# Two transformer blocks on one core: reordering the end of the first stage, with part of the next stage's modulation sums on GpSimd

## The chip, the cores and the metric

The kernel runs on one core of one Trainium2 chip. The metric is the device time of one execution in microseconds (us), given as the median of three runs; shorter is better. PE is TensorE, PEld its weight loads, DVE VectorE, ACT ScalarE, POOL GpSimd, SP SyncE (here only a queue of DMAs).

## The reference, cut to what matters

A block of a token mixer and a SwiGLU feed-forward, then a second model of two layers with three sublayers each, on 256 tokens of width 1024, all in f32. Each of the eight sublayers is modulated by a vector computed from `c`: shift, scale and gate are `silu(c) @ w_ada + b_ada`. The part that the change touches is the first sublayer, from its convolution and its attention to the layer norm behind it, and the modulation vector of the second:

```python
u = gate_c * hc
conv = sum(conv_w[j] * pad(u)[:, j:j + s, :] for j in range(3))
conv_out = group_rms_norm(gate_b * conv, conv_norm_g, 8)
attn = group_rms_norm(sparse_indexer_attention(q, k, v, qi, ki, wi, 64), attn_norm_g, 8)
mix = concat([attn, conv_out]) @ w_out
x = layer_norm(2**0.25 * x + g1 * mix, ln1_g, ln1_b)
ff = swiglu(modulate(x, sh2, sc2), w_gate, w_up, w_down)      # sh2, sc2 = part of silu(c) @ w_ada
```

## The kernel before, in words

The whole program is one launch of eight stages, `s` = 0 to 7, one for each sublayer. Every engine has its own instruction stream, written out by hand in the order in which it runs; semaphores alone tie the streams together. There is no planner.

Weights stream through a ring of three slots of 128x2048 f32 (a unit). SP loads a unit into `raw`, ACT rounds it to `whi` (`hi`, L674), DVE takes the rest into `wlo` (`lo`, L1294), and PE multiplies three times for each product (`three`, L2157: high by high, high by low, low by high). The inputs are split in the same way into `hhi` and `hlo`. A unit may be loaded once the `lo` three units before it is done. Stage 0 has 14 units, called U to U+13 here; U+10 to U+13 are the output projection `w_out`, each with 24 matmuls of 512 columns, 12 for each half of the tokens (t = 0 and 1).

The modulation vector of stage 1 (its shift and scale) and the gate of stage 0 are summed outside PE: 24 pieces (128 rows of `w_ada`, 1024 columns each) are loaded by POOL (`early_piece`, L551 to L557) into five slots in turn, and DVE multiplies each by a column of `silu(c)` and adds it to `ada_acc` (`early_piece`, L1619 to L1628, one instruction of 128x1024). Pieces 0 to 7 belong to the gate, 8 to 23 to stage 1. The semaphore `a_used` counts finished pieces; a piece's slot is loaded again when the piece five before it is done. At the end PE adds up the 128 rows of `ada_acc` with a matrix of ones (`sum_gate`, `sum_columns`, L2165: 16 column sums, 32 PE instructions), once all 24 pieces are in.

The end of stage 0 runs as follows.

- DVE forms `u` (L1752, `conv_u`) when PE has finished unit U+9. ACT multiplies it by the last tap (L1245, `conv_tap`), DVE adds the other two taps in a chain of eight instructions (L1761) and multiplies by the gate (L1763, `conv_gated`), ACT squares (L1250, `conv_sq`), PE sums the groups (L2850, `group_mm`), DVE scales (L1768, `block_mean`), POOL takes the inverse root (`inverse_root`, L494, `block_root`), PE turns it (L2856), ACT copies it (L1255, `group_out`), PE spreads it over the features (L2862, `spread_mm`), and DVE normalises (L1780, `mix_f`).
- Beside that the attention ends. PE turns the softmax weights (`turn_weights`, L2817), ACT and DVE copy them out (L1219, L1739), PE multiplies by the values (`attend(t)`, L2827), ACT squares (L1214), DVE sums and takes the means (`heads_out`), POOL the inverse root, DVE normalises (`heads_norm`, L1731), PE turns (the transposes in front of `output_product`, L2282), and DVE multiplies by the gain (L1787, `mix_f`).
- Each third of the mixed input is split by ACT (L712) and DVE (L1347). PE then runs `output_product`: unit U+10 for both t, then, in `close`, `sum_gate(0)`, U+11 to U+13 for t = 0, then U+11 to U+13 for t = 1. `sum_columns(1)` follows.
- DVE in `leave_first` (L1414): multiplies by the gate and takes the moments of t = 0 (L1356, L1371, L1376), adds pieces 21 to 23, runs `lo` of the next stage's first unit, sets the columns of stage 1 (L1325 to L1328) when PE has summed them, modulates, and does t = 1.

`keep_busy(n, b)` (L2151) issues n matmuls of ones into bank b, two PE instructions each; their result is not used.

Of the kernel before, what the change touches and what calls it, by code (L numbers as in the profile page):

```python
# [26 lines left out]
ALU = mybir.AluOpType  # L27
# [124 lines left out]
def two_blocks(  # L152
# [30 lines left out]
    with ExitStack() as ctx:  # L183
# [146 lines left out]
        q_copied, vg_out, lv_sub, lv_exp, lv_mul = sem("q_copied"), sem("vg_out"), sem("lv_sub"), sem("lv_exp"), sem("lv_mul")  # L330
        lv_mm, lv_copy, g_silu = sem("lv_mm"), sem("lv_copy"), sem("g_silu")
        lv_far, o_scaled = sem("lv_far"), sem("o_scaled")
        mean_eps, hi_first, lo_first = sem("mean_eps"), sem("hi_first"), sem("lo_first")

        def linked(engine, own):
# [155 lines left out]
        def _(pool):  # L491
# [101 lines left out]
            for s in range(NSUB):  # L593
# [11 lines left out]
                if s == 0:  # L605
                    pool.wait_ge(f_used, 13)
                    pool.wait_ge(w_hi, 2)
                    pool.wait_ge(cols_sum, 1)
                    for n in range(13):
                        early_piece(n)  # L610
                    pool.wait_ge(block_mean, 1)
                    inverse_root(st[:, 40:56], 16, block_root)
                    early_piece(13)
                    pool.wait_ge(block_mean, 2)
                    inverse_root(st[:, 120:128], 8, block_root)
                    early_piece(14)
                    pool.wait_ge(block_mean, 3)
                    inverse_root(st[:, 128:136], 8, block_root)
                    for n in range(15, EARLY):
                        early_piece(n)  # L620
                elif s == 1:

                    pool.wait_ge(toe_rows, 1)
                    pool.dma_start(bias_row[:, :], big[0:HEADS, 2560:2560 + TOE]).then_inc(toe_land, 16)
                elif s == 2:

                    rows = big[:, 3072:3072 + HEADS * TOE]
                    ada_pieces(s, 0, 5)
                    pool.wait_ge(toe_land, 48)
                    pool.dma_start(rows, bias_row.rearrange("h j -> (h j)").unsqueeze(0).to_broadcast((P, HEADS * TOE))).then_inc(toe_land, 16)  # L630
                    ada_pieces(s, 5, 6)
                    pool.wait_ge(toe_land, 64)
                    pool.dma_start(bias_rows[:, :, :], rows.rearrange("p (h j) -> p h j", h=HEADS)).then_inc(toe_land, 16)
                    ada_pieces(s, 6, 7)
                    pool.wait_ge(toe_land, 80)
                    skewed = bass.AP(tensor=bias_rows.tensor, offset=bias_rows.offset + P - 1,
                                     ap=[[HEADS * TOE - 1, P], [TOE, HEADS], [1, TOK]])
                    pool.dma_start(big[:, 6144:8192].rearrange("p (h k) -> p h k", h=HEADS), skewed).then_inc(toe_land, 16)
                    ada_pieces(s, 7, KT)
# [25 lines left out]
        def _(sc):  # L665
# [572 lines left out]
            exps(0)  # L1238
            hi(U + 11)
            exps(1)  # L1240
            take_turned(0)
            sc.wait_ge(conv_u, 1)
            sc.wait_ge(w_used, used(U + 7))
            for ct in range(4):
                done = sc.activation(hf[:, ct, :], big[:, D + ct * TOK:D + (ct + 1) * TOK], ACT.Copy,  # L1245
                                     scale=vec[:, V_CW + 8 + ct:V_CW + 9 + ct])
            done.then_inc(conv_tap, 1)
            square_heads_out(0)
            sc.wait_ge(conv_gated, 1)
            sc.activation(hfl[:, 0:D], hfl[:, D:2 * D], ACT.Square).then_inc(conv_sq, 1)  # L1250
            take_turned(1)
            square_heads_out(1)
            hi(U + 12)
            sc.wait_ge(group_tr, 1)
            sc.activation(act[0:8, 0, 0:TOK], ps[0:8, 1, 0:TOK], ACT.Copy).then_inc(group_out, 1)  # L1255
            split_mixed(1, 4, 4, 0, TOK)
            for t in range(NT):
                split_mixed(2 + t, 0, 4, t * P, P)
# [18 lines left out]
        def _(ve):  # L1277
# [468 lines left out]
            choose(1)  # L1746
            logits(0)
            lo(U + 9)
            logits(1)
            ve.wait_ge(w_used, used(U + 9))  # L1750
            ve.wait_ge(hc_out, 1)
            ve.tensor_tensor(big[:, D:2 * D], big[:, 0:D], bank(2, 2), ALU.mult).then_inc(conv_u, 1)  # L1752
            early_piece(7)
            lo(U + 10)
            early_piece(8)

            ve.wait_ge(conv_tap, 1)
            for ct in range(4):
                for j in (1, 2):
                    w = V_CW + 4 * (2 - j) + ct  # L1760
                    link(ve.scalar_tensor_tensor(cv[:, ct, j:TOK], u[:, ct, 0:TOK - j], vec[:, w:w + 1], cv[:, ct, j:TOK],  # L1761
                                                 ALU.mult, ALU.add))
            ve.tensor_tensor(hfl[:, D:2 * D], hfl[:, 0:D], bank(0, 2), ALU.mult).then_inc(conv_gated, 1)  # L1763
            early_piece(9)
            pt_evac(1)
            early_piece(10)
            ve.wait_ge(group_mm, 1)
            ve.tensor_scalar(st[:, 40:56], ps[:, 0, 0:16], 1.0 / 64, EPS1, ALU.mult, ALU.add).then_inc(block_mean, 1)  # L1768
            heads_out(0)
            early_piece(11)  # L1770
            lo(U + 11)
            early_piece(12)
            heads_out(1)
            heads_norm(0)
            early_piece(13)
            heads_norm(1)

            ve.wait_ge(spread_mm, 1)
            for ct in range(4):
                done = ve.scalar_tensor_tensor(hf[:, 4 + ct, :], hf[:, 4 + ct, :], vec[:, V_CG + ct:V_CG + ct + 1],  # L1780
                                               psf[:, ct * TOK:(ct + 1) * TOK], ALU.mult, ALU.mult)
            done.then_inc(mix_f, 1)
            early_piece(14)
            split_mixed(1, 4, 4, 0, TOK)
            for t in range(NT):
                ve.wait_ge(o_tr, t + 1)
                ve.tensor_tensor(hf[:, 0:4, t * P:(t + 1) * P], ps[:, 4 + t, :].rearrange("p (k n) -> p k n", k=4),  # L1787
                                 vec[:, V_AG:V_AG + 4].unsqueeze(2).to_broadcast((P, 4, P)), ALU.mult).then_inc(mix_f, 1)
                split_mixed(2 + t, 0, 4, t * P, P)
            ve.wait_ge(lam_exp, 1)  # L1790
            link(ve.tensor_tensor(st[:, 220:221], st[:, 219:220], st[:, 218:219], ALU.subtract))
            link(ve.tensor_scalar(st[:, 221:222], st[:, 220:221], -LAMBDA_INIT, None, ALU.add))
            lo(U + 12)
            for n in range(15, 19):
                early_piece(n)
            lo(U + 13)
            early_piece(19)
            early_piece(20)
            leave_first()

            def attention():
# [345 lines left out]
        def _(pe):  # L2147
# [110 lines left out]
            def close(s, places, before):  # L2258

                last = len(places) - 1  # L2260
                for j, place in enumerate(places):
                    before(j, 0)
                    done = rows_of(*place, 0, False, j == last, signal=y_ready if j == last else None)
                done.then_inc(y_ready, 1)
                for j, place in enumerate(places):
                    turning = (lambda: transpose_inputs(s + 1, 0)) if j == last and s in (2, 4, 5) else None
                    before(j, 1)
                    if j == last and s in (3, 6):
                        transpose_inputs(s + 1, 0)
                    rows_of(*place, 1, False, j == last, signal=y_ready if j == last else None,  # L2270
                            between=turning).then_inc(w_used, 1)
                if s == 0:
                    sum_columns(1)
                if s == 1:
                    sum_columns(2)
                if s < 2:
                    transpose_inputs(s + 1, 0)
# [32 lines left out]
            def output_product(s, unit, mixed_ready, k0=0, beside=None):  # L2310
# [10 lines left out]
                        pe.wait_ge(mix_lo, mixed_ready[j, t])  # L2321

                def before(j, t):
                    if s == 0 and (j, t) == (0, 0):
                        pe.wait_ge(mix_f, 3)
                        sum_gate(0)
                    mixed(j + 1, t)
# [490 lines left out]
                                            logit_rows(t)[:, h, g * P:(g + 1) * P], ident)  # L2818
                done.then_inc(p_tr, 1)

            def attend(t):
                pe.wait_ge(pt_s, t + 1)
                if t:
                    pe.wait_ge(pt_v, 1)
                for h in range(HEADS):
                    for g in range(t + 1):
                        done = pe.matmul(ps[:, (2, 6)[t], h * 64:(h + 1) * 64], PT[:, g, h * P:(h + 1) * P],  # L2827
                                         tok[:, g, VO:VO + 64], start=g == 0, stop=g == t)
                done.then_inc(pv_mm, 1)

            pe.wait_ge(qT_out, 1)
            logit_products(0)
# [6 lines left out]
            keep_busy(4, 4)  # L2839
            pe.wait_ge(conv_u, 1)  # L2840
            turn_weights(0)
            keep_busy(5, 5)
            attend(0)
            turn_weights(1)
            keep_busy(8, 3)

            pe.wait_ge(conv_sq, 1)
            for t in range(NT):
# [1 line left out]
                    done = pe.matmul(ps[:, 0, 8 * t + 2 * ct:8 * t + 2 * ct + 2], hf[:, ct, t * P:(t + 1) * P],  # L2850
                                     kc[:, C_HALF:C_HALF + 2], start=True, stop=True)
            done.then_inc(group_mm, 1)
            attend(1)
            pe.wait_ge(block_root, 1)
            for t in range(NT):
                done = pe.transpose(ps[0:8, 1, t * P:(t + 1) * P], st[:, 40 + 8 * t:48 + 8 * t], ident)  # L2856
            done.then_inc(group_tr, 1)
            keep_busy(7, 3)
            pe.wait_ge(group_out, 1)
            pe.wait_ge(spread_land, 16)  # L2860
            for ct in range(4):
                done = pe.matmul(psf[:, ct * TOK:(ct + 1) * TOK], gate[0:8, 1, ct * P:(ct + 1) * P], act[0:8, 0, 0:TOK],  # L2862
                                 start=True, stop=True)
            done.then_inc(spread_mm, 1)
            for t in range(NT):
                pe.wait_ge(o_done, t + 1)
                transposes([big[:, 3920 + BANK * t + j * P:3920 + BANK * t + (j + 1) * P] for j in range(4)], 4 + t, o_tr)
            output_product(0, U + 10, {(0, 0): 1, (2, 0): 2, (2, 1): 3}, 4)

            for s in range(1, NSUB):  # L2870
                if s in SWIGLUS:
# [28 lines left out]
```

## Time and profile before

| | |
|---|---|
| median of 3 runs | 1447.03 us (1443.84 to 1448.16) |
| the profiled execution | 1452.88 us |
| its span, first to last instruction | 1451.2 us |
| mean granted TensorE clock | 0.979 |
| busy: PE / PEld / DVE / ACT / POOL | 1414.5 / 1184.0 / 1051.4 / 705.8 / 180.4 us |

The change touches the stretch from about 97 us to about 183 us of the span. The busy share of an engine is a mean over the whole span, and eight stages behind that stretch are the same code before and after. So the page serves to find the stretch, and the chain of waits, the timelines of the engines and the clock within it say what a change there is worth.

### The profile page before, as it was taken

The numbers are of one execution on the slowest core, as the hardware profiler recorded it, in microseconds if no ns is written. First come the engines' busy times: TensorE is split into PE (matmuls) and PEld (weight loads), VectorE is DVE, ScalarE is ACT, GpSimd is POOL, SyncE is SP. The second block draws the span as 40 slices with busy tenths as digits, with TensorE's granted clock in tenths as the row PEclk, the third lists the DMA queues.
The fourth block names the chain that finished last, engine by engine and source line by source line (L and its number), as shares of the span: only waits on it lengthen the run. The fifth ranks groups of instructions, "written<-read, shape, count | busy, mean of one in ns | idle before, by whom it ended". The sixth has DMA issues, their size and how long they took to land.

```text
span 1451.2 us, 19791 instructions
## 1 busy us (share of the span) xinstructions
PE 1414.5 (97%) x7136; PEld 1184.0 (82%) x7136; DVE 1051.4 (72%) x1105; ACT 705.8 (49%) x936; POOL 180.4 (12%) x272
## 2 busy tenths in 40 slices
PE   8998999999999999999999999999999999999998
PEld 8897778888788887768788887788888988788887
DVE  5888867776768877686667775688866888665555
ACT  2453354444634335667734345534338856644342
POOL 3103111110301210211101101111101001100000
PEclk7996999999999999999999999999999999999999
DMA  9846479897389995443578983899955342466661
GB/s 356 317 146 203 146 240 307 307 312 255 118 292 349 367 361 192 149 156 107 194 269 313 316 280 113 287 336 343 344 184 180 117 140 88 131 205 227 222 228 59
DMA packets 187526, 335.62 MB, mean 231 GB/s; under 512 B 9169, under 2 KB 123453, under 8 KB 187216
## 3 DMA queue, kind: packets, MB, share of 16 engines
q1 hardware_dynamic: 160528, 237.95, 48.7%
q0 software_dynamic: 26736, 96.71, 18.4%
q8 instruction: 35, 0.57, 0.2%
q10 hardware_dynamic: 208, 0.23, 0.0%
q14 instruction: 19, 0.16, 0.0%
HBM read 332.23 MB, written 2.63 MB: 231 GB/s over the span
## 4 chain that ended last, share of the span: by engine, by line
PE 78%; DVE 10%; issue 4%; ACT 3%; DMA 3%; POOL 1%; SPq 1%; DVEq 0%; ACTq 0%; POOLq 0%
PE ps L2157 68%; DMA raw<-in_ffn_w_in 2%; DVE wlo L1294 2%; PE ps L2165 1%; PE ps L2351 1%; PE ps L2612 1%; PE ps L2282 1%; DVE ada_acc L1627 1%; DMA big<-in_w_ada 1%; DVE xn L1356 1%; ACT whi L674 1%; POOL st L494 1%; PE ps L2296 1%; ACT hf L699 1%; DVE xs L1361 1%
## 5 line engine op out<-in xcount | busy, mean ns | idle before, releaser
L1294 DVE TENSOR_TENSOR wlo<-raw,whi 128x2048 fp32r<-128x2048 f32 x203 | 463.3, 2285 | 145.0 <-ACT whi L674 143.7
L2157 PE MATMUL ps<-whi,hhi 128*128 128x512 f32 (+1 forms) x1208 | 490.8, 406 | 13.3 <-DVE hlo L1347 4.2
L674 ACT ACTIVATE whi<-raw 128x2048 fp32r<-128x2048 f32 x208 | 396.4, 1909 | 218.0 <-PE ps L2157 163.9
L2157 PE MATMUL ps<-whi,hlo 128*128 128x512 f32 (+1 forms) x1208 | 475.5, 394 | 0.0
L2157 PE MATMUL ps<-wlo,hhi 128*128 128x512 f32 (+1 forms) x1208 | 474.7, 393 | 0.0
L2157 PEld LDWEIGHTS ps<-whi,hhi 128*128 128x128 f32 x1208 | 229.8, 190 | 67.0 <-issue 8.2
L2157 PEld LDWEIGHTS ps<-whi,hlo 128*128 128x128 f32 x1208 | 229.4, 190 | 49.6
L2157 PEld LDWEIGHTS ps<-wlo,hhi 128*128 128x128 f32 x1208 | 230.2, 191 | 45.1 <-issue 1.7
L2157 PE MATMUL ps<-whi,ahi 128*128 128x512 f32 x400 | 156.2, 390 | 0.7 <-DVE alo L1514 0.7
L2157 PE MATMUL ps<-whi,alo 128*128 128x512 f32 x400 | 155.7, 389 | 0.0
L2157 PE MATMUL ps<-wlo,ahi 128*128 128x512 f32 x400 | 155.6, 389 | 0.0
L1309 DVE SCALAR_TENSOR_TENSOR ada_acc<-ada_raw,csil,ada_acc 128x1024 f32<-128x1024 f32 x104 | 130.3, 1278 | 0.0
L527 POOL DMA_DIRECT2D ada_raw<-in_ada_w x96 | 51.1, 532 | 542.9 <-DVE ada_acc L1309 531.3
L792 ACT ACTIVATE ahi<-ps 128x512 fp32r<-128x512 f32 x50 | 29.9, 599 | 181.7 <-PE ps L2351 181.7
L788 ACT ACTIVATE act<-ps 128x256 f32<-128x256 f32 x110 | 42.1, 384 | 146.7 <-PE ps L2157 146.5
L1514 DVE TENSOR_TENSOR alo<-ps,ahi 128x512 fp32r<-128x512 f32 x50 | 34.6, 692 | 88.9 <-ACT ahi L792 88.8
L2157 PEld LDWEIGHTS ps<-whi,ahi 128*128 128x128 f32 x400 | 75.1, 188 | 16.5 <-DVE wlo L1294 1.1
L2157 PEld LDWEIGHTS ps<-whi,alo 128*128 128x128 f32 x400 | 75.1, 188 | 15.6
L2157 PEld LDWEIGHTS ps<-wlo,ahi 128*128 128x128 f32 x400 | 75.1, 188 | 15.4
L494 POOL TENSOR_TENSOR st<-st 128x1 f32<-128x1 f32 (+3 forms) x35 | 41.7, 1192 | 205.1 <-DVE st L1393 64.6
L1509 DVE TENSOR_TENSOR act<-act,ps 128x256 f32<-128x256 f32 x110 | 42.7, 416 | 29.8 <-ACT act L788 29.6
L2157 PE MATMUL ps<-hhi,whi 128*128 128x256 f32 x224 | 64.2, 287 | 0.0
(288 smaller groups left out, 1496.5 us busy)
## 6 DMA issues: line engine op xcount, KB each, us to landing
raw<-in_ffn_w_in SPq DMA_DIRECT2D x176, 512.0 KB
ada_raw<-in_ada_w POOLq DMA_DIRECT2D x96, 512.0 KB, 5.2
raw<-in_ffn_w_down SPq DMA_DIRECT2D x44, 1024.0 KB
big<-in_ada_w POOLq DMA_DIRECT2D x48, 512.0 KB, 6.2
raw<-in_hgrn_w_in SPq DMA_DIRECT2D x16, 1024.0 KB
raw<-in_attn_w_qkv SPq DMA_DIRECT2D x12, 1024.0 KB
ada_raw<-in_w_ada POOLq DMA_DIRECT2D x23, 512.0 KB, 4.9
raw<-in_w_gate SPq DMA_DIRECT2D x22, 512.0 KB
```

What stands on the lines that cost most here:

```text
L494: pool.tensor_tensor(cols, cols, half.to_broadcast((P, width)), ALU.pow).then_inc(signal, 1)
L527: pool.dma_start(ada_slot(p), w[bass.ds(kt * P, P), first + j * D:first + (j + 1) * D])\
L674: sc.activation(whi[:, slot, 0:n], raw[:, slot, 0:n], ACT.Copy).then_inc(w_hi, 1)
L699: done = sc.activation(hf[:, kt, toks], ps[:, 2 * t + kt // 4, kt % 4 * P:(kt % 4 + 1) * P], ACT.Identity, scale=modc[:, s % 2, 8 + kt:9 + ...
L788: sc.activation(act[:, t, :], ps[:, 4 + t, 0:FC], ACT.Silu).then_inc(silu_done, 1)
L792: sc.activation(ahi.rearrange("p k n -> p (k n)"), bank(6), ACT.Copy).then_inc(ahi_ready, 1)
L1294: ve.tensor_tensor(wlo[:, slot, 0:n], raw[:, slot, 0:n], whi[:, slot, 0:n].bitcast(F32), ALU.subtract)\
L1309: ve.scalar_tensor_tensor(acc, ada_slot(p), csil[:, bass.ds((0 if a < 2 else 8) + kt, 1)], acc, ALU.mult, ALU.add).then_inc(a_used, 1)
L1356: link(ve.tensor_tensor(xn[:, t, cols], bank(2 * t + h), gate[:, s % 2, cols], ALU.mult))
L1509: ve.tensor_tensor(act[:, t, :], act[:, t, :], ps[:, 4 + t, FC:2 * FC], ALU.mult).then_inc(act_ready, 1)
L1514: ve.tensor_tensor(a_lo, bank(6), a_hi.bitcast(F32), ALU.subtract).then_inc(alo_ready, 1)
L2157: done = pe.matmul(dst, lhsT, rhs, start=first and n == 0, stop=final and n == 2, skip_group_check=True)
```

## The change

In stage 0's end and in the step to stage 1:

1. DVE. Pieces 7 and 8 move ahead of the forming of `u`, to either side of `logits(1)`. The chain of taps follows `lo(U+10)` at once, and waits for each of ACT's four taps by itself. Piece 9 moves behind the copy of the turned weights, piece 10 behind `heads_out(0)`, piece 12 behind the normalised convolution, where it was 14. `heads_out(1)`, `heads_norm(1)` and the second third of the input move behind the split of the convolution's part. `lo(U+12)` moves between the two steps of the last third. Pieces 17 to 20 leave DVE.
2. POOL. It issues the load of piece 13 before it waits for the first mean, and 14 and 15 one step earlier too. Behind its three inverse roots it issues 16 to 21, and then multiplies and adds pieces 17, 18, 19 and 20 itself, in two instructions each (a product in place, then a sum, with a semaphore between), issuing the loads of 22 and 23 between them.
3. ACT. The four taps come before the copy of the first turned weights; the squares for t = 1 come behind `group_out`; the copy of the second turned weights comes before the convolution's square.
4. PE. `turn_weights(1)` comes before `attend(0)`; `attend(1)` is cut in two, four heads before and four behind the spreading; three groups of `keep_busy` go or change size (5, 8 and 7 matmuls out, 10 in); `keep_busy(5)` is new in front of `sum_columns(1)`.
5. PE. The output product starts once the heads of t = 0 are turned. The heads of t = 1 are turned between U+10 and U+11, and `sum_gate(0)` moves from before U+11 to before U+12.

```diff
@@ gpsimd
-                    for n in range(13):
+                    for n in range(14):
                         early_piece(n)
                     pool.wait_ge(block_mean, 1)
                     inverse_root(st[:, 40:56], 16, block_root)
-                    early_piece(13)
+                    early_piece(14)
                     pool.wait_ge(block_mean, 2)
                     inverse_root(st[:, 120:128], 8, block_root)
-                    early_piece(14)
+                    early_piece(15)
                     pool.wait_ge(block_mean, 3)
                     inverse_root(st[:, 128:136], 8, block_root)
-                    for n in range(15, EARLY):
+                    for n in range(16, 22):
                         early_piece(n)
+                    for n in range(17, 21):
+                        pool.wait_ge(a_land[n % EARLY_SLOTS], 16 * (n // EARLY_SLOTS + 1))
+                        pool.wait_ge(a_used, n)
+                        kt, j = divmod(n - KT, 2)
+                        acc = ada_acc[:, 1, j * D:(j + 1) * D]
+                        pool.tensor_scalar(early_slot(n % EARLY_SLOTS), early_slot(n % EARLY_SLOTS), csil[:, kt:kt + 1], None,
+                                           ALU.mult).then_inc(piece_scaled, 1)
+                        pool.wait_ge(piece_scaled, n - 16)
+                        pool.tensor_tensor(acc, acc, early_slot(n % EARLY_SLOTS), ALU.add).then_inc(a_used, 1)
+                        if n + EARLY_SLOTS < EARLY:
+                            early_piece(n + EARLY_SLOTS)
@@ scalar
             exps(1)
-            take_turned(0)
             sc.wait_ge(conv_u, 1)
             sc.wait_ge(w_used, used(U + 7))
             for ct in range(4):
-                done = sc.activation(hf[:, ct, :], ...)
-            done.then_inc(conv_tap, 1)
+                sc.activation(hf[:, ct, :], ...).then_inc(conv_tap, 1)
+            take_turned(0)
             square_heads_out(0)
+            take_turned(1)
             sc.wait_ge(conv_gated, 1)
             sc.activation(hfl[:, 0:D], hfl[:, D:2 * D], ACT.Square).then_inc(conv_sq, 1)
-            take_turned(1)
-            square_heads_out(1)
             hi(U + 12)
             sc.wait_ge(group_tr, 1)
             sc.activation(act[0:8, 0, 0:TOK], ps[0:8, 1, 0:TOK], ACT.Copy).then_inc(group_out, 1)
+            square_heads_out(1)
             split_mixed(1, 4, 4, 0, TOK)
@@ vector
             lo(U + 9)
+            early_piece(7)
             logits(1)
+            early_piece(8)
             ...
             ve.tensor_tensor(big[:, D:2 * D], big[:, 0:D], bank(2, 2), ALU.mult).then_inc(conv_u, 1)
-            early_piece(7)
             lo(U + 10)
-            early_piece(8)
-            ve.wait_ge(conv_tap, 1)
             for ct in range(4):
+                ve.wait_ge(conv_tap, ct + 1)
                 ...
+            pt_evac(1)
             early_piece(9)
-            pt_evac(1)
-            early_piece(10)
             ve.wait_ge(group_mm, 1)
             ...
             heads_out(0)
+            early_piece(10)
             early_piece(11)
             lo(U + 11)
-            early_piece(12)
-            heads_out(1)
             heads_norm(0)
-            early_piece(13)
-            heads_norm(1)
             ve.wait_ge(spread_mm, 1)
             ...
-            early_piece(14)
+            early_piece(12)
             split_mixed(1, 4, 4, 0, TOK)
-            for t in range(NT): (L1787 and split_mixed of t)
+            heads_out(1)
+            turned_heads(0)
+            early_piece(13)
+            split_mixed(2, 0, 4, 0, P)
+            heads_norm(1)
+            early_piece(14)
+            early_piece(15)
+            turned_heads(1)
+            lo(U + 12)
+            split_mixed(3, 0, 4, P, P)
             ...
-            lo(U + 12)
-            for n in range(15, 19):
-                early_piece(n)
+            early_piece(16)
             lo(U + 13)
-            early_piece(19)
-            early_piece(20)
             leave_first()
@@ tensor
                 if s == 0:
+                    keep_busy(5, column_bank(1))
                     sum_columns(1)
@@
-                    if s == 0 and (j, t) == (0, 0):
+                    if s == 0 and (j, t) == (1, 0):
                         pe.wait_ge(mix_f, 3)
                         sum_gate(0)
@@
             turn_weights(0)
-            keep_busy(5, 5)
-            attend(0)
             turn_weights(1)
-            keep_busy(8, 3)
+            pe.wait_ge(pt_s, 1)
+            attend(0, range(HEADS)).then_inc(pv_mm, 1)
+            keep_busy(10, 3)
             ...
-            attend(1)
+            attend(1, range(4))
             pe.wait_ge(block_root, 1)
             ...
-            keep_busy(7, 3)
             pe.wait_ge(group_out, 1)
             ...
             done.then_inc(spread_mm, 1)
-            for t in range(NT): (wait for o_done, transposes)
-            output_product(0, U + 10, {(0, 0): 1, (2, 0): 2, (2, 1): 3}, 4)
+            attend(1, range(4, HEADS)).then_inc(pv_mm, 1)
+            turn_heads_out(0)
+            output_product(0, U + 10, {(0, 0): 1, (2, 0): 2, (2, 1): 3}, 4, beside_first)
```

`beside_first` calls `turn_heads_out(1)` at (1, 0), before U+11 of t = 0; `turned_heads(t)` is the wait for the turned heads and L1787.

## Rows read from the trace of the kernel before

**Rows 1.** The page's part 4, the chain that ended last, by engine.

```profile
PE 78%; DVE 10%; issue 4%; ACT 3%; DMA 3%; POOL 1%; SPq 1%; DVEq 0%; ACTq 0%; POOLq 0%
```

**Rows 2.** Chain of waits, 118 to 199 us: start, us, engine, tile, line, count.

```profile
118.62 1.23 DVE hf L1763
...
119.88 1.06 ACT hf L1250
...
120.99 3.03 PE ps L2850 x16
124.02 6.93 PE ps L2827 x32
...
131.37 2.99 PE ps L2151 x14
134.36 3.72 PE ps L2862 x8
...
167.76 3.85 PE ps L2165 x32
...
183.07 15.48 PE ps L2157 x60
```

**Rows 3.** Timeline of DVE; in brackets the idle time before and its releaser.

```profile
108.74 1.22 DVE L1752 TENSOR_TENSOR big<-big,ps 128x1024 f32<-128x1024 f32 x1 [1.25 <-PE ps L2157]
...
111.08 2.28 DVE L1294 TENSOR_TENSOR wlo<-raw,whi 128x2048 fp32r<-128x2048 f32 x1
...
114.48 4.11 DVE L1761 SCALAR_TENSOR_TENSOR hf<-big,vec,hf 128x255 f32<-128x255 f32 x8
...
138.10 1.66 DVE L1780 SCALAR_TENSOR_TENSOR hf<-hf,vec,ps 128x256 f32<-128x256 f32 x4 [1.95 <-PE ps L2862]
...
159.58 0.69 DVE L1371 SCALAR_TENSOR_TENSOR xs<-xs,xn 128x512 f32<-128x512 f32 x1
...
166.42 1.28 DVE L1627 SCALAR_TENSOR_TENSOR ada_acc<-ada_acc,csil 128x1024 f32<-128x1024 f32 x1
```

**Rows 4.** Timeline of ACT, same columns.

```profile
112.38 1.69 ACT L1245 ACTIVATE hf<-big,vec 128x256 f32<-128x256 f32 x4
...
130.98 0.60 ACT L1214 ACTIVATE xn<-ps 128x512 f32<-128x512 f32 x1 [9.13 <-PE ps L2827]
...
139.79 1.06 ACT L712 ACTIVATE hhi<-hf 128x1024 fp32r<-128x1024 f32 x1 [6.16 <-DVE hf L1780]
```

**Rows 5.** Timeline of PE, same columns.

```profile
112.53 2.00 PE L2827 MATMUL ps<-big 128*128 128x64 f32 x16 [0.30 <-ACT big L1219]
...
116.12 1.95 PE L2151 MATMUL ps<-ones 128*128 128x128 f32 x16
...
142.17 0.79 PE L2157 MATMUL ps<-whi,hhi 128*128 128x512 f32 x1 [2.20 <-DVE hlo L1347]
...
167.19 0.39 PE L2157 MATMUL ps<-whi,hlo 128*128 128x512 f32 x1
```

**Rows 6.** Windows: us, busy of PE, PEld, DVE, ACT, POOL; PEclk, DMA share, GB/s.

```profile
120.00:130.00 10.00, 9.01 (x45) 9.01 (x46) 9.18 (x12) 1.85 (x2) 5.65 (x3) 0.58 0.48 141
130.00:140.00 10.00, 9.97 (x37) 8.04 (x36) 6.21 (x16) 2.86 (x4) 4.96 (x7) 0.50 0.84 279
140.00:150.00 10.00, 7.83 (x26) 6.14 (x27) 8.41 (x10) 2.54 (x4) 0.53 (x1) 0.72 0.47 163
```

**Rows 7.** Timeline of POOL, 124 to 181 us, columns as for DVE.

```profile
124.31 2.94 POOL L494 TENSOR_TENSOR st<-st 128x16 f32<-128x16 f32 x1 [12.33 <-DVE st L1768]
...
163.70 1.60 POOL L494 TENSOR_TENSOR st<-st 128x1 f32<-128x1 f32 x1 [8.74 <-DVE st L1393]
165.40 1.03 POOL L582 TENSOR_SCALAR st<-st 128x1 f32<-128x1 f32 x1
...
179.76 0.56 POOL L494 TENSOR_TENSOR st<-st 128x1 f32<-128x1 f32 x1 [13.34 <-DVE st L1393]
```

**Rows 8.** Groups of POOL by line and shape: busy us, mean ns, idle before.

```profile
L512 POOL MEMSET ada_acc<- 128x1024 f32 x1 | 1.0, 957 | 0.0
```

More of the change, by code:

```diff
@@ L332, in two_blocks @@
         lv_far, o_scaled = sem("lv_far"), sem("o_scaled")
+        piece_scaled = sem("piece_scaled")
         mean_eps, hi_first, lo_first = sem("mean_eps"), sem("hi_first"), sem("lo_first")
@@ L1244, in _ @@
             for ct in range(4):
-                done = sc.activation(hf[:, ct, :], big[:, D + ct * TOK:D + (ct + 1) * TOK], ACT.Copy,
-                                     scale=vec[:, V_CW + 8 + ct:V_CW + 9 + ct])
-            done.then_inc(conv_tap, 1)
+                sc.activation(hf[:, ct, :], big[:, D + ct * TOK:D + (ct + 1) * TOK], ACT.Copy,
+                              scale=vec[:, V_CW + 8 + ct:V_CW + 9 + ct]).then_inc(conv_tap, 1)
+            take_turned(0)
             square_heads_out(0)
+            take_turned(1)
             sc.wait_ge(conv_gated, 1)
             sc.activation(hfl[:, 0:D], hfl[:, D:2 * D], ACT.Square).then_inc(conv_sq, 1)
-            take_turned(1)
-            square_heads_out(1)
             hi(U + 12)
@@ L1782, in _, with turned_heads @@
             done.then_inc(mix_f, 1)
-            early_piece(14)
+            early_piece(12)
             split_mixed(1, 4, 4, 0, TOK)
-            for t in range(NT):
+            def turned_heads(t):
                 ve.wait_ge(o_tr, t + 1)
@@ L1788, in _ @@
                                  vec[:, V_AG:V_AG + 4].unsqueeze(2).to_broadcast((P, 4, P)), ALU.mult).then_inc(mix_f, 1)
-                split_mixed(2 + t, 0, 4, t * P, P)
+            heads_out(1)
[8 more added lines that the diff above has]
+            split_mixed(3, 0, 4, P, P)
             ve.wait_ge(lam_exp, 1)
@@ L2819, in turn_weights, with attend @@
                 done.then_inc(p_tr, 1)
[L2821 to L2825, printed above, removed]
+            def attend(t, heads):
+                for h in heads:
                     for g in range(t + 1):
@@ L2828, in attend @@
                                          tok[:, g, VO:VO + 64], start=g == 0, stop=g == t)
-                done.then_inc(pv_mm, 1)
+                return done
             pe.wait_ge(qT_out, 1)
@@ L2852, in _ @@
             done.then_inc(group_mm, 1)
-            attend(1)
+            pe.wait_ge(pt_s, 2)
+            pe.wait_ge(pt_v, 1)
+            attend(1, range(4))
             pe.wait_ge(block_root, 1)
@@ L2864, in _, with turn_heads_out, beside_first @@
             done.then_inc(spread_mm, 1)
-            for t in range(NT):
+            attend(1, range(4, HEADS)).then_inc(pv_mm, 1)
+            def turn_heads_out(t):
                 pe.wait_ge(o_done, t + 1)
                 transposes([big[:, 3920 + BANK * t + j * P:3920 + BANK * t + (j + 1) * P] for j in range(4)], 4 + t, o_tr)
-            output_product(0, U + 10, {(0, 0): 1, (2, 0): 2, (2, 1): 3}, 4)
+            def beside_first(j, t):
+                if (j, t) == (1, 0):
+                    turn_heads_out(1)
+            turn_heads_out(0)
+            output_product(0, U + 10, {(0, 0): 1, (2, 0): 2, (2, 1): 3}, 4, beside_first)
             for s in range(1, NSUB):
```

## The prediction

> **What bounds the kernel now.** The chain of waits is read first. Over the whole span it is PE for 78% [rows 1], so a change counts only where PE waits or runs slowly. The stretch that the change rewrites holds both. From 118.6 to 140 us the chain alternates: gate product on DVE, square on ACT, group sums, the second `attend` (6.93 us), `keep_busy` (2.99) and the spreading (3.72) on PE [rows 2], then the normalising on DVE, for which it had waited 1.95 us [rows 3]. Second, the windows: the granted clock is 0.58 in 120 to 130 us, 0.50 (1.2 GHz) in 130 to 140 and 0.72 in 140 to 150 [rows 6]. It fell after PE had been idle between the end of its `keep_busy` at 118.07 and 120.99, and rose 3.1 us into the output product. Third, PE's own timeline: the output product starts at 142.17, after 2.20 us of waiting for DVE's split [rows 5], and ends at 167.58. Its 96 matmuls fill that time without a gap. Fourth, DVE: the last of its 24 pieces starts at 166.42 and ends at 167.70 [rows 3], and the column sums follow at 167.76 [rows 2]. That is the point that matters most: PE and DVE reach the column sums within 0.12 us of each other. Starting PE's product earlier gains nothing unless the 24 pieces are in earlier too. From the column sums' start at 167.76 to PE's steady work of the next stage at 183.07 [rows 2] it is 15.3 us, by code that the change leaves alone; so the whole change is worth what it moves the column sums, and what clock they find.
>
> **Part by part, on the profiled execution's own times.** It took 1452.88 us, its span and 1.7 us around it, 5.85 us over the median of the runs; differences found on it are applied to the median.
>
> *Convolution's chain.* Piece 7 goes where DVE waited for logits, piece 8 into the 1.25 us of idle before `u` [rows 3]; one lasts 1.28 us, overlapping the next by some 0.08, so both are free and `u` stays at 108.74. `lo(U+10)` then runs 109.9 to 112.1, and the chain of taps follows at 112.1 instead of 114.48. ACT's four taps take 1.69 us [rows 4] from the end of its exponentials at 111.5, the first ready at 111.9, so they are hidden. Four microseconds of chain, 1.2 of gate product, 1.06 of square: the square ends at 118.6, not 120.94. Gain so far 2.3 us. PE then does its group sums: 16 instructions that took 3.03 us at a falling clock [rows 2], 1.9 taken: 120.5.
>
> *To the spreading.* The mean, then POOL's root of 16 columns (2.94 us [rows 7]) to 123.7. Four heads of `attend` lie beside it instead of eight in front of it: that removes the 6.93 us, and the `keep_busy` of 2.99 is gone too. Turn 0.43 and ACT copy 0.36: spreading from 124.6. At half clock it lasts 3.72 [rows 2], to 128.35. I take half clock: group sums of two columns, four heads of 64 columns and waiting are all that PE does from 118.6 to 124, and in the trace the clock fell in such a stretch and did not rise again under 6.93 us of `attend`, nor under the `keep_busy` and spreading behind it [rows 6].
>
> *To the product.* DVE meanwhile does `heads_out(0)`, pieces 10 and 11, `lo(U+11)` and `heads_norm(0)`, to 127.8, so the spreading is what it waits for. Normalising 1.66 [rows 3] to 130.0. What is late next is a wait that ACT's new order adds: the squares of t = 1 stand in front of ACT's split, and they need the last four heads of `attend`, 16 instructions at 6.93/32 = 0.217 us, so 131.85. Squares 0.60, split 1.06 [rows 4], DVE's split 1.2: the product starts at 134.7, 7.5 us earlier than 142.17.
>
> *Product.* U+10 at half clock for its first 3 to 4 us as before, 7.1 us, to 141.9; heads of t = 1 turned (`heads_norm(1)` is done by 139.5), 1.0 us, to 143.0. DVE: gain on the turned heads to 143.7, `lo(U+12)` to 145.9, split to 146.6, lambda, piece 16 to 148.15, `lo(U+13)` to 150.3. PE does U+11 of t = 0, the gate sum, U+12, and waits for `lo(U+13)` about 0.7 us. U+13 ends for t = 0 at 153.1, and 36 matmuls at 8.15 us end the product at 161.3, 6.3 us earlier than 167.58. The new `keep_busy(5)` is 10 instructions at 1.95/16 = 0.12 us [rows 5]: 162.5.
>
> *Pieces on GpSimd.* POOL gets to them when piece 16 is done, since the load of 21, queued in front of them, waits for that: 148.15, and 0.55 for the load. The trace shows no POOL instruction of 128x1024 that reads. The nearest row is a memset of that shape, 0.957 us [rows 8], one stream. Multiplying reads one stream and writes one: 0.96 if they run together, 1.9 if in turn; I take 1.1, nearest to the memset. Adding reads two and writes one: 0.96 to 2.9; I take 1.9, two reads in turn with the write beside them. A semaphore from POOL to POOL costs 0.1 (from the end of the root at 163.70 to the next at 165.40 [rows 7]), twice. A piece is 3.2 us, bounds 2.1 and 5.0, against 1.4 on DVE.
> The Trainium skill, GPSIMD Engine Reference, section 3.1, has a two-input add of 2048 columns at 4497 ns, so an estimate of 2.25 us for 1024; no row here shows one. By it the sum would be 1.4 us later.
> POOL also meets DVE: a root of one column took 0.56 us with DVE idle and 1.60 with DVE in a piece [rows 7]. So the first product waits for `lo(U+13)` to end, 150.3, and the moments of t = 0 may cost it 0.4 more. Four pieces 12.8, two loads 1.1: 164.6. Then DVE adds 21 to 23, which must come after piece 20: 3 x 1.28 and two handovers, 4.2. All are in at 168.8, 1.1 us later than 167.70. DVE, relieved of four pieces, stands idle for some 8 us, and so does PE from 162.5.
>
> *Clock of the column sums.* With PE idle for 6 us the clock falls, as it did after 2.9. The column sums take 3.85 us at full clock [rows 2]; at half, by 2.99/14 = 0.214 us for each of 32, 6.85. Bounds 0 and +3.0; I take +1.8, a rise after about 3.1 us as in the output product. Behind them the chain's 11.4 us stay.
>
> Sum: +1.1 + 1.8 = **+2.9 us**: 1455.8 for the profiled execution, 1449.9 on the median, +0.2%.
>
> **Rivals.**
> *A, GpSimd keeps up.* A piece in 2.1 us ends POOL at 160.2 and the pieces at 164.4; with less waiting behind DVE and piece 16 done earlier, PE's 162.5 is the bound, and the clock holds. Gain 167.76 - 162.5 = 5.3: 1441.8. For it: the memset's rate. Against: an add reads twice what a memset writes.
> *B, GpSimd and DVE exclude each other (the opposite side: slower).* The 1.60 against 0.56, and the multiply-add of one column at 1.03 [rows 7], are waits for a running DVE instruction to end. If a POOL instruction of 2 us then holds DVE off as well, `lo(U+13)` or the moments' instructions (0.69 each [rows 3]) and POOL's eight alternate, 0.5 us for each of the eight, 4 in all, and the column sums are wholly at half clock: 1.1 + 4.0 + 3.0 = +8.1, 1455.1. It decides once a piece on POOL costs over 3.6 us. Against it: DVE has only some 7 us of work between 150 and 165.
> The Trainium skill, SBUF — State Buffer, section "SBUF: two separate sides", states such an exclusive lock for instructions with two SBUF inputs; the 1.60 agrees for POOL behind DVE, the other direction no row shows.
> *C, the clock stays up before the product.* Spreading 1.9 instead of 3.72, eight half-heads 1.8 instead of 3.5 (by 2.00 for 16 [rows 5]): the product starts at 132.0 and piece 16 ends some 3.7 us earlier, and all else too: 2.9 - 3.7 = -0.8, 1446.2. Against: two-column sums did not hold the clock.
>
> **Numbers.** Forecast 0.40, A 0.24, B 0.22, C 0.14. What a measurement can tell from no change is about 0.3%, 4.3 us. The forecast's own range, by the bounds of a piece and of the clock, is 1444 to 1454, of which 0.08 lies beyond +4.3. Faster: A without its weaker part (0.20), C at its best (0.04): 0.24. Slower: B and 0.08: 0.30. Same: 0.46. The range for 8 in 10 runs from A's 1441 to B's 1455.5.
>
> **What would show it.** Chain of taps starting at 112.1; group sums at 118.6; spreading at half clock, 124.6 to 128.4; ACT's split of the convolution behind the squares of t = 1; product from about 134.7 to 161.3; POOL's first product near 150.3, its pairs 3.2 us apart; a hole on PE of about 6 us before the column sums, and these at half clock. Wrong it would be if pairs are near 2 us or above 4, if piece 16 ends well away from 148, or if the clock does not fall where I have it fall.

## The result, and the profile after

The changed kernel takes 1462.38 us in the median of four runs (1461.54 to 1463.30), the kernel before 1447.60 beside it (1443.84 to 1448.78): ratio 1.0096, 95% interval [1.0079, 1.0113], 14.8 us slower by the medians, 13.9 by the ratio. The forecast was +2.9 us, no measurable change; the side was that of rival B, and the time lies beyond the range.

| | before | after |
|---|---|---|
| median of runs | 1447.60 us | 1462.38 us |
| profiled execution, its span | 1452.88, 1451.2 us | 1462.96, 1461.3 us |
| output product starts | 142.17 us | 135.00 us |
| all 24 pieces in | 167.70 us | 177.88 us |
| column sums start, busy | 167.76, 3.85 us | 177.92, 6.23 us |
| steady work of stage 1 from | 183.07 us | 195.60 us |

The chain of waits after, from the end of the convolution's chain to stage 1 (start us, us, engine, tile, line, count). To the column sums it is no longer PE and DVE, but POOL, whose instructions follow each other from 148 us to 173.6:

```profile
117.32 1.07 ACT hf L1262
...
118.43 1.96 PE ps L2863 x16
...
124.72 3.78 PE ps L2876 x8
128.50 3.62 PE ps L2840 x16
...
132.14 0.60 ACT xn L1226
132.74 0.95 ACT hhi L724
...
148.78 4.09 POOL ada_raw L627
...
152.95 2.68 POOL ada_acc L630
...
171.25 2.35 POOL ada_acc L630
...
173.73 1.30 DVE ada_acc L1638
...
177.92 6.23 PE ps L2180 x32
...
195.60 13.90 PE ps L2172 x60
```

POOL's own timeline, with shapes. L627 is the product, L630 the sum. Two rows matter most. The second product, 2.87 us, has beside it on DVE the end of one instruction of 128x512 and two of one or two columns. The second sum, 2.38 us, has nothing beside it. So these are the prices of the two instructions with DVE out of the way. The first product has 4.08; counted from the end of DVE's `lo(U+13)` at 150.13 it is 2.73, so its time reads as a wait for that instruction:

```profile
148.78 4.08 POOL L627 TENSOR_SCALAR ada_raw<-ada_raw,csil 128x1024 f32<-128x1024 f32 x1
152.95 2.68 POOL L630 TENSOR_TENSOR ada_acc<-ada_acc,ada_raw 128x1024 f32<-128x1024 f32 x1
155.92 0.63 POOL L557 DMA_DIRECT2D ada_raw<-in_w_ada  x1 [0.30 <-POOL ada_acc L630]
156.59 2.87 POOL L627 TENSOR_SCALAR ada_acc<-ada_acc,csil 128x1024 f32<-128x1024 f32 x1
159.55 2.38 POOL L630 TENSOR_TENSOR ada_acc<-ada_acc 128x1024 f32<-128x1024 f32 x1
...
168.32 2.84 POOL L627 TENSOR_SCALAR ada_raw<-ada_raw,csil 128x1024 f32<-128x1024 f32 x1 [0.17 <-POOL ada_acc L630]
171.25 2.34 POOL L630 TENSOR_TENSOR ada_acc<-ada_acc,ada_raw 128x1024 f32<-128x1024 f32 x1
```

DVE's timeline of the same stretch shows the other side: 16.39 us of idle that POOL's last sum ends, and one instruction (L1382 at 154.85) of 1.33 us. The same line takes 0.69 at 152.67. POOL's first sum was running until 155.63, which is 0.55 before the longer one ends, so it reads as a wait for that sum. The two between them ran at their usual 0.69 beside the same sum; one reads a single tile from SBUF, the other one from there and one from PE's result banks (`ps`). SBUF is where the other tiles lie:

```profile
147.84 2.29 DVE L1305 TENSOR_TENSOR wlo<-raw,whi 128x2048 fp32r<-128x2048 f32 x1
...
152.67 0.69 DVE L1382 SCALAR_TENSOR_TENSOR xs<-xs,xn 128x512 f32<-128x512 f32 x1
153.40 0.69 DVE L1387 BATCH_NORM_STATS2 st<-xs 128x6 f32<-128x512 f32 x1
154.12 0.69 DVE L1367 TENSOR_TENSOR xn<-ps,gate 128x512 f32<-128x512 f32 x1
154.85 1.33 DVE L1382 SCALAR_TENSOR_TENSOR xs<-xs,xn 128x512 f32<-128x512 f32 x1
...
173.73 2.71 DVE L1638 SCALAR_TENSOR_TENSOR ada_acc<-ada_raw,csil,ada_acc 128x1024 f32<-128x1024 f32 x2 [16.39 <-POOL ada_acc L630]
```

PE after, the product's first matmul and the two groups on either side of the hole (columns as in [rows 5]); then the window of the hole, where the granted clock is 0.62 (columns as in [rows 6]):

```profile
135.00 0.80 PE L2172 MATMUL ps<-whi,hhi 128*128 128x512 f32 x1 [2.04 <-DVE hlo L1358]
...
161.20 1.28 PE L2166 MATMUL ps<-ones 128*128 128x128 f32 x10
177.92 6.21 PE L2180 MATMUL ps<-ones,ada_acc 128*128 128x128 f32 x32 [15.44 <-DVE ada_acc L1638]
```

```profile
162.00:178.00 16.00, 0.56 (x6) 0.37 (x4) 3.99 (x4) 1.52 (x2) 12.44 (x7) 0.62 0.11 33
```

On the profiled executions the account closes. The column sums start 10.2 us later and take 2.4 us more; stage 1's first 60 matmuls take 13.90 instead of 15.48 us [rows 2], 1.6 less; 0.9 more comes back behind them, in code that is the same. Sum: 10.1, the difference of the spans.

The medians differ by 14.8. The profiled execution of before lay 5.3 us above its median, that of after 0.6. Of the 4.7 between these two, some 3.8 are found. The unchanged code in e2's trace, below, reaches `lo(U+12)` at 144.14 us instead of 146.38: 0.6 earlier ahead of the stretch, 1.1 in the group sums (1.95 against 3.03), 0.5 in `attend`. The other 1.6 are stage 1's first matmuls. They are no effect of the change: e6 and e6 again are one kernel, with column sums of 3.85 us in both, and the 60 matmuls take 15.50 in one and 13.91 in the other. Such steps change from one execution to the next with the granted clock.

One more of them bears on every start time below. The same 120 matmuls of L2157, from 43.3 to 44.8 us on, take 23.48 us in before and 23.59 in after, 22.08 in e2, but 20.7 to 20.8 in all the other traces. So before and after enter the stretch at about the same time (DVE's reduction for `logits(1)` starts at 105.20 and 104.95), e2 at 104.58, and the others at 101.9 to 102.8.

### The profile page after: what moved, and what is told of

It reads as the page before. It is cut to its first block, busy times and chain, and to the rows that moved or that the text cites. A ratio compares the mean times of both kernels' runs of the same rounds, so it can differ in the third digit from the quotient of the medians.

```text
span 1461.3 us, 19778 instructions
## 1 busy us (share of the span) xinstructions
PE 1411.3 (97%) x7126; PEld 1180.5 (81%) x7126; DVE 1047.0 (72%) x1101; ACT 706.0 (48%) x936; POOL 200.8 (14%) x280
## 4 chain that ended last, share of the span: by engine, by line
PE 78%; DVE 9%; issue 4%; ACT 4%; POOL 3%; DMA 3%; ACTq 0%; DVEq 0%; SPq 0%; POOLq 0%
PE ps L2172 67%; DVE wlo L1305 2%; DMA raw<-in_ffn_w_in 2%; PE ps L2180 2%; PE ps L2367 1%; PE ps L2298 1%; PE ps L2628 1%; POOL st L495 1%; ACT whi L686 1%; DVE xn L1367 1%; PE ps L2312 1%; ACT hf L711 1%; POOL ada_acc L630 1%; PE ps L2166 1%; PE ps L2726 1%
## 5 line engine op out<-in xcount | busy, mean ns | idle before, releaser
L2172 PEld LDWEIGHTS ps<-wlo,ahi 128*128 128x128 f32 x400 | 75.1, 188 | 15.5
L2172 PE MATMUL ps<-hhi,wlo 128*128 128x256 f32 x224 | 63.3, 283 | 0.0
```

Of the source, the lines that this page charges most:

```text
L2172: done = pe.matmul(dst, lhsT, rhs, start=first and n == 0, stop=final and n == 2, skip_group_check=True)
```

## The experiments

**e1: pieces 17 to 20 back on VectorE.**

```diff
-                    (GpSimd's loop over pieces 17 to 20)
+                    for n in range(16, EARLY):
+                        early_piece(n)
@@ vector
             lo(U + 13)
+            for n in range(17, 21):
+                early_piece(n)
             leave_first()
```

> The changed kernel with pieces 17 to 20 back on VectorE, behind lo(U+13); all of the new order is kept. Theory P (the price of a piece on GpSimd, some 5.2 us for its two instructions with VectorE idle, sets the end): VectorE is then busy from 150 us on with four pieces, the moments and three pieces, all 24 are in at about 164.6 us, and the column sums start there instead of at 177.9. About 3 us faster than the kernel before, ratio 0.998, and 13 us less than the changed kernel. Rival O (the new order itself costs the time, by the clock and by waits): the ratio stays above 1.004. Rival L (GpSimd and VectorE hold each other off) expects what P expects here; the dose in e3 tells them apart.

Measured: 1445.83 us, ratio to before 0.9989 [0.9975, 1.0003]. The column sums start at 162.71 at full clock, 5.0 us earlier than before; 3.0 of these it had already when it entered the stretch (DVE's reduction at 102.16), so 2.0 are the new order's. The medians give 1.6, about half of the 3 expected, and the interval reaches to no gain. The new order by itself costs nothing; the whole loss, 16.5 us between the medians of this kernel and the changed one, hangs on the four pieces.

```profile
162.71 3.85 PE ps L2171 x32
...
178.01 13.90 PE ps L2163 x60
```

**e2: the kernel before, with the four pieces on GpSimd and nothing else.** Its edit is the loop over 17 to 20 of the diff in POOL's stream, and `early_piece(17)` to `(20)` taken out of DVE's.

> The kernel before with nothing changed but that GpSimd does pieces 17 to 20. P: piece 16 is done at about 151.4 us, GpSimd takes 4 x 5.4 us and two loads, to 176, VectorE adds three pieces, and the column sums start at about 180.5 instead of 167.8, at half clock: 13 + 2.4 = 15 us slower than before, ratio 1.0105. O: not more than half of the changed kernel's loss, ratio below 1.005.

Measured: 1462.00 us, ratio 1.0088 [1.0063, 1.0114], 14.5 us. The chain of waits:

```profile
120.36 1.95 PE ps L2860 x16
...
179.11 6.27 PE ps L2175 x32
```

The pieces alone carry all of the changed kernel's loss, and the new order beside them gains nothing that the medians show (1462.0 and 1462.4): what it gains on PE ends in the wait for POOL. Rival O falls.

**e3: one piece on GpSimd.** As the changed kernel, with POOL's loop over piece 17 alone and DVE's pieces 18 to 23 behind the moments.

> The changed kernel with only piece 17 on GpSimd; VectorE does 18 to 20 with 21 to 23, behind the moments. P: GpSimd is done with piece 17 at about 155.7 us, while VectorE has the moments of t = 0 to do until 157.3, so the piece is hidden; six pieces of 1.4 us then end at 165.7. Ratio to before 0.999, some 12 us less than the changed kernel. If the cost lay in the contention with the moments (L), the moments, which lie beside this one piece, would keep most of the loss: contention is 1.6 us in the changed kernel's trace, and it would have to be much more.

Measured: 1450.22 us, ratio 1.0015 [1.0001, 1.0028]: 12.2 us less than the changed kernel, as expected, but 4.4 more than e1, where 1.1 was expected. The trace shows part of it. The piece is in at 153.3, under the moments, but the column sums start at 163.44 (e1: 162.71) and take 5.48 us instead of 3.85: PE's product had ended 0.6 us earlier than in e1, the pieces 0.7 later, PE waited 3.25 us instead of 1.91, and the clock had fallen. Both traces enter the stretch at 102.2. The rest of the 4.4 is not found.

```profile
146.50 4.08 POOL L627 TENSOR_SCALAR ada_raw<-ada_raw,csil 128x1024 f32<-128x1024 f32 x1
150.66 2.67 POOL L630 TENSOR_TENSOR ada_acc<-ada_acc,ada_raw 128x1024 f32<-128x1024 f32 x1
```

```profile
163.44 5.48 PE ps L2180 x32
```

**e4: four forms of GpSimd's product.** For 18, 19 and 20 in place of the `tensor_scalar` by `csil[:, kt:kt + 1]`:

```diff
+ 18: pool.tensor_tensor(slot, slot, csil[:, kt:kt + 1].to_broadcast((P, D)), ALU.mult)
+ 19: pool.tensor_scalar(slot, slot, 1.5, None, ALU.mult)
+ 20: the tensor_scalar in two halves of 512 columns
```

> The product on GpSimd in four forms, one for each piece: 17 as in the change, 18 as a product of two inputs with the column broadcast, 19 with an immediate 1.5 in place of the column (so this piece has another factor), 20 in two instructions of 512 columns. If the product's 2.85 us is the price of a scalar taken from memory, 19 is near 1.0 to 1.3 us; if it is the price of that instruction's loop at this width, 19 is 2.8 and each half of 20 about 1.45; if two inputs are served faster than a scalar pointer, 18 is about 2.35 like the sum.

Measured, in one run of 1461.52 us, POOL's timeline (products only):

```profile
154.54 1.92 POOL L631 TENSOR_TENSOR ada_acc<-ada_acc,csil 128x1024 f32<-128x1024 f32 x1
...
159.86 2.79 POOL L633 TENSOR_SCALAR ada_acc<-ada_acc 128x1024 f32<-128x1024 f32 x1
...
165.24 1.56 POOL L635 TENSOR_SCALAR ada_raw<-ada_raw,csil 128x512 f32<-128x512 f32 x1 [0.18 <-POOL ada_acc L639]
166.79 1.56 POOL L636 TENSOR_SCALAR ada_raw<-ada_raw,csil 128x512 f32<-128x512 f32 x1
```

The scalar from memory is not the cost (2.79 without it). The price goes with the width: 1.56 for 512, 2.85 for 1024, so by estimate about 2.5 ns a column and 0.3 us beside. The product of two inputs, one a broadcast column, is the cheaper form.

**e5: the clock held.** `keep_busy(5, ...)` in front of the column sums becomes `keep_busy(66, ...)`.

> The changed kernel with keep_busy(66) instead of keep_busy(5) in front of the column sums, so that TensorE works through the 15.4 us in which it waited. Theory: the clock then stays at 2.4 GHz, the 32 instructions of the column sums take 3.85 us instead of 6.23, and the kernel is 2.4 us shorter than the changed one, ratio to before 1.008. Rival (the late column sums cost nothing more than their lateness, because something behind them absorbs the 2.4 us): no shorter.

Measured: 1460.46 us (1458.74 to 1463.86), ratio 1.0088 [1.0065, 1.0110]. That is 1.9 us less than the changed kernel, but the two intervals overlap, so the time alone decides nothing. In the trace the column sums are back at 3.85 us, the 2.4 expected. Stage 1's first matmuls take 15.51 instead of 13.90 in this execution. That is not shown to be a price of the held clock: e1 has column sums of 3.85 and 13.90 behind them, e8 5.69 and 15.51.

```profile
175.28 3.85 PE ps L2180 x32
...
190.58 15.51 PE ps L2172 x60
```

**e7: the cheaper product for all four pieces.** The changed kernel with e4's form of 18 throughout.

> The changed kernel with GpSimd's product of all four pieces written as a product of two inputs, the column broadcast (1.92 us in e4's trace instead of 2.85). Theory P: the pieces lie in series, so the column sums come 4 x 0.93 = 3.7 us earlier than in the changed kernel; ratio to before 1.007. Rival L (the pace is set by contention with VectorE): less than 1 us earlier.

Measured: 1456.57 us, ratio 1.0059 [1.0039, 1.0079], 5.8 us less than the changed kernel. The sums stay at 2.34 to 2.74 us, and the products are 1.9 but for the first, 3.11 behind `lo(U+13)`:

```profile
158.51 1.91 POOL L627 TENSOR_TENSOR ada_acc<-ada_acc,csil 128x1024 f32<-128x1024 f32 x1
160.49 2.34 POOL L630 TENSOR_TENSOR ada_acc<-ada_acc 128x1024 f32<-128x1024 f32 x1
```

Not less than 1 us, as rival L had it: the pieces' own price sets the end. Counted from DVE's reduction for `logits(1)`, the column sums start 69.5 us on and not 73.0, 3.5 earlier, close to the 3.7 expected; why the medians differ by 5.8 is not found. The loss goes from 14.8 to 9.0 us.

**e8: the product written to another place.** `gate[:, 1, :]` takes the product; 17 and 18 as `tensor_scalar`, 19 and 20 with two inputs.

> The changed kernel with GpSimd's product written to another place than it is read from (an unused row of gate), pieces 17 and 18 with the scalar from memory, 19 and 20 with two inputs. If writing in place is what makes the product 2.85 us, 17 (less the wait for lo) and 18 fall to 1.0 to 1.5 us; if it is the instruction's own pace, they stay at 2.85 and the two-input form at 1.92.

Measured, in one run of 1458.95 us: piece 18's product 2.87, piece 19's 1.91 us. Writing in place costs nothing.

```profile
153.80 2.87 POOL L628 TENSOR_SCALAR gate<-ada_acc,csil 128x1024 f32<-128x1024 f32 x1
156.75 2.38 POOL L634 TENSOR_TENSOR ada_acc<-ada_acc,gate 128x1024 f32<-128x1024 f32 x1
...
160.06 1.91 POOL L631 TENSOR_TENSOR gate<-ada_acc,csil 128x1024 f32<-128x1024 f32 x1
```

**e6: e1 with ACT's split of the convolution before the squares of t = 1.**

```diff
-            square_heads_out(1)
             split_mixed(1, 4, 4, 0, TOK)
+            square_heads_out(1)
```

> e1 with one line moved: ScalarE splits the convolution's part before it squares the heads of t = 1. In e1 the split stands behind the squares, which wait for the last four heads, and VectorE is idle for some 2.3 us ahead of its own split. Theory: TensorE then starts the product about 1.5 us earlier, when it has turned the heads of t = 0, VectorE is ahead by 2 us, and the column sums start 1.5 to 2 us earlier than in e1: ratio to before 0.9975. Rival: VectorE and TensorE meet again at lo(U+13) and the turned heads, and nothing is gained.

Measured: 1444.06 us, ratio 0.9979 [0.9962, 0.9995]. The column sums start at 159.59, and DVE, all busy, is still the one that PE waits for. This is faster than both kernels, by 0.2% of the kernel before.

```profile
159.59 3.85 PE ps L2171 x32
...
174.88 15.50 PE ps L2163 x60
```

**e9 and e6 again: one piece where DVE has other work.** e6 with piece 16 on POOL, in e4's cheaper form, between DVE's pieces 15 and 17.

> e6 with one piece, 16, on GpSimd, with two-input products, while VectorE has the last third of the input, lo(U+12) and lo(U+13) to do between pieces 15 and 17. Theory: the piece takes 1.9 + 2.35 us and two waits for VectorE's lo, some 6 to 7 us in all, inside the 8 us that VectorE has other work; VectorE loses a piece of 1.2 to 1.4 us, and the column sums start about 1 us earlier than in e6. Rival L: GpSimd's sum and lo(U+12) or lo(U+13) hold each other off, VectorE loses up to 2.3 us by it, and e9 is 1 us or more longer than e6.

> The same kernel as e6_split_first, beside e9 on the same chip: ratio to before 0.998, column sums 2 to 3 us earlier than in e1.

Measured on the same chip: e6 again 1442.92 us, ratio 0.9956 [0.9943, 0.9969]; e9 1446.31, ratio 0.9985 [0.9969, 1.0001]: 3.4 us longer than e6 again. The theory's +1 us of gain falls; rival L's outcome came. In e6 again the column sums start 4.4 us earlier than in e1, more than the 2 to 3 expected:

```profile
158.28 3.85 PE ps L2171 x32
...
173.58 13.91 PE ps L2163 x60
```

In e9 they start at 161.66. POOL's two instructions:

```profile
137.94 1.91 POOL L625 TENSOR_TENSOR ada_raw<-ada_raw,csil 128x1024 f32<-128x1024 f32 x1
139.93 4.33 POOL L627 TENSOR_TENSOR ada_acc<-ada_acc,ada_raw 128x1024 f32<-128x1024 f32 x1
```

and DVE beside them, where `lo(U+12)` takes 3.93 instead of 2.28 us and the split (L1355) 2.88 instead of 0.69:

```profile
138.08 3.93 DVE L1302 TENSOR_TENSOR wlo<-raw,whi 128x2048 fp32r<-128x2048 f32 x1
141.93 2.88 DVE L1355 TENSOR_TENSOR hlo<-hf,hhi 128x512 fp32r<-128x512 f32 x1
```

DVE lost 3.8 us to save a piece of 1.3, and PE waited 2.29 us for `lo(U+13)`. Taken with their undisturbed times, the instructions ran one after another: `lo` went on when the product ended (139.85), POOL's sum when `lo` ended (142.0), the split when the sum ended (144.26).

## Why the prediction was wrong

*Convolution's chain, spreading, start of the product.* Right, each step within 0.3 us. The chain of taps started at 111.8 (forecast 112.1), the group sums at 118.4 (118.6), the spreading at 124.7 at half clock (124.6), ACT's split behind the squares at 132.7 (132.5), the product at 135.0 (134.7). `lo(U+13)` ended at 150.1 (150.3), the product at 161.2 (161.3). That the start times agree so well is in part luck: the trace of before, on which they were worked out, and that of after had both lost 2.7 us in the 120 matmuls ahead of the stretch, and most others had not. The distances hold without it: from DVE's reduction for `logits(1)` to the product it is 30.0 us in after and in e1, 29.5 in the forecast.

*Pieces on GpSimd.* This is the step that failed, by the size of one term. A piece was put at 3.2 us with 2.1 and 5.0 as bounds; it costs 5.2 in its two instructions, some 5.5 with its handovers. The product was put at 1.1 by the memset [rows 8], at most 1.9 for a read and a write in turn, and takes 2.85: the bound itself was wrong, for it took an instruction's pace on POOL to be that of its streams, and e4 and e8 show that it goes by the form of the instruction. Four products: 7.0 us. The sum was put at 1.9 and takes 2.35: 1.8 us. Together 8.8 of the 9.1 us by which the pieces came in later than forecast (177.9 and 168.8). The rest is small and partly cancels: each of the two loads between the pieces cost 0.95 us with its handovers, not 0.55, and the handovers inside the pieces less than was put. That this term decides the time is shown by e1, e2 and e7. The Trainium skill's figure for the sum, 2.25 us by the estimate from GPSIMD Engine Reference, section 3.1, is close to the 2.34 to 2.38 of the trace; the memset was the worse guide.

*The range.* It was also drawn too narrow for its own bounds. A piece at 5.0 us is 4 x 1.8 = 7.2 us more, and the clock's upper bound 1.2 more: 2.9 + 8.4 = +11.3, 1458.3, where the prediction has 1454 for these bounds and ends its range at 1455.5. The measured 1462.4 lies beyond both, since a piece costs more than its upper bound.

*The clock of the column sums.* Forecast +1.8, measured +2.4 (6.23 us), within the bounds.

*The base.* The sum was made on an execution 5.3 us above its own median, with the difference carried over whole. Some 3.8 us of that, mostly clock, the code of before does not lose in every execution, so the difference on the medians is 14.8, and that on the profiles 10.1. Even that is far more than the +2.9 forecast.

*Rival B* had the side right and the price wrong in kind. It put 4 us on POOL and DVE holding each other off. In the changed kernel holding off costs about 1.6 us on POOL (1.2 behind `lo`, 0.3 behind the moments) and 0.64 on DVE, as DVE has little to do from 150 to 173 us. Where both have work, e9, it is 3.8 us for one piece: the mechanism is real, and more costly than B had it. Its point of decision, 3.6 us for a piece on POOL, was passed by the uncontended price alone.

*Rival A* fell with the price of a piece. *Rival C* did not occur: the spreading (3.78 us) and the last four heads (3.67) ran at half clock. Only the group sums (1.95) and part of the first four heads (2.53), which lie beside POOL's root, had more.

## What to carry to other kernels

Moving work to an idle engine pays only if that engine's chain, at its own price, ends before the one that it relieves: here four pieces went from 5.6 us on a busy engine to 24.8 us in series on an idle one, and the relieved engine stood idle for 16.4 of them, behind pieces that had to come last. Price such a move by the form of the instruction, not by another that moves as many bytes, and measure it by itself first if no row shows it. And take the change apart: the reordering that came with it, kept alone and with one wait mended, beats both kernels, by 0.2 to 0.4% of the kernel before (e6, twice).

## What the runs showed of the hardware

- On GpSimd, f32, 128x1024, with VectorE idle: `tensor_scalar` product 2.79 to 2.87 us, with a scalar from memory or an immediate, in place or not; `tensor_tensor` product with a broadcast column 1.89 to 1.92; `tensor_tensor` sum 2.34 to 2.41. A memset of the shape had 0.96 [rows 8].
- GpSimd and VectorE hold each other off in both directions when VectorE's instruction reads two tiles from SBUF: POOL's sum 4.33 instead of 2.34 us, DVE's `lo` 3.93 instead of 2.28, a 128x512 subtraction 2.88 instead of 0.69, with times that add up as if they ran in turn (e9). VectorE's instructions with one tile from SBUF kept their 0.69 us beside POOL's first sum in the changed kernel. The Trainium skill, SBUF — State Buffer, section "SBUF: two separate sides", has this as an exclusive lock held for a whole instruction, against VectorE where it has two SBUF inputs; these rows agree.
- The kernel before is spread by 9 us between executions (1443.8 to 1452.9), and part of that is where the clock falls: between traces the same 16 group sums took 3.03 and 1.95 us, the same 60 matmuls 15.5 and 13.9, the same 120 matmuls 23.5 and 20.7.
